# The opening of the first mixer: filter taps before the pool products, four small loads on ScalarE's queue, window sums by level, bias row added in the taps

## The reference, cut to what matters

```python
def pool_mixer(h, w, scale):                  # first mixer; h is the normed input
    for g, win in enumerate((2, 4, 8, 16)):   # 4 groups of 256 channels
        xg = hf[..., g * 256:(g + 1) * 256]
        cs = jnp.cumsum(xg, axis=1)
        lag = jnp.pad(cs[:, :-win], ((0, 0), (win, 0), (0, 0)))
        cnt = jnp.minimum(pos + 1, win)
        outs.append((cs - lag) / cnt - xg)
    pooled = jnp.stack(outs, axis=2)
    return jnp.einsum('blgc,gcd->blgd', pooled, w).reshape(B, L, 1024) * scale

def hyena_filters(L, w1, b1, w2, b2, freq, w3):   # depends on weights alone
    hid = jnp.sin(fr * (z @ w1 + b1))
    hid = jnp.sin(fr * (hid @ w2 + b2))
    h = (hid @ w3).reshape(L, 2, 2, 512)
    return h * decay[:, None, None, :]

def long_conv_bidir(u, h_fwd, h_bwd, bias):
    k2 = jnp.concatenate([h_fwd, zeros, h_bwd[:0:-1]], axis=0)
    K = jnp.fft.rfft(k2, n=2 * L, axis=0)         # the filter's spectrum
    ...
    return y + u * bias
```

## Time and profile before

| | us |
|---|---|
| median of 3 runs | 1048.89 (1047.71 to 1049.81) |
| the profiled execution | 1046.43 |
| its span, first to last instruction | 1044.7 |
| TensorE busy | 1004.6 (96%) |
| VectorE busy | 764.4 (73%) |
| ScalarE busy | 497.5 (48%) |
| GpSimd busy | 139.1 (13%) |
| mean granted clock | 0.985 |

### The profile page before, as it was taken

The page is one execution under the profiler, slowest core; times in us unless marked ns, Lnnn a source line. Parts: engine busy times, 40 slices in busy tenths (PEclk is TensorE's granted clock), DMA queues, the critical chain, the costliest instruction groups (busy, mean ns, idle before and its releaser), DMA issues.

```text
span 1044.7 us, 20358 instructions
## 1 busy us (share of the span) xinstructions
PE 1004.6 (96%) x7736; PEld 943.4 (90%) x7736; DVE 764.4 (73%) x1223; ACT 497.5 (48%) x728; POOL 139.1 (13%) x153
## 2 busy tenths in 40 slices
PE   5999999999999998999999999999999999999996
PEld 4379999999999988999999998987788999999996
DVE  6669888888866657998867765766455879866554
ACT  6355544444645534454444432564446555554441
POOL 4000000012000036300015400111110330000111
PEclk9699999999999998999999999999999999999998
DMA  7048777667733334566635632442233548644552
GB/s 250 1 161 290 264 271 259 204 240 246 251 123 122 122 104 159 201 240 238 229 127 192 228 127 86 164 145 91 100 123 122 185 176 296 249 163 173 167 178 84
DMA packets 38493, 186.80 MB, mean 179 GB/s; under 512 B 4936, under 2 KB 8809, under 8 KB 25578
## 3 DMA queue, kind: packets, MB, share of 16 engines
q1 hardware_dynamic: 38442, 186.09, 51.2%
HBM read 185.03 MB, written 1.05 MB: 178 GB/s over the span
## 4 chain that ended last, share of the span: by engine, by line
PE 87%; DVE 7%; ACT 2%; issue 2%; POOL 1%; DMA 0%; SPq 0%; DVEq 0%; ACTq 0%
PE ps L415 25%; PE ps L417 25%; PE ps L416 25%; DVE wl L356 2%; PE ps L1729 1%; PE ps L1997 1%; PE ps L1948 1%; PE ps L1738 1%; PE ps L1969 1%; PE ps L1957 1%; PE ps L1773 1%; PE ps L2022 1%; PE ps L2008 1%; DVE xl L1209 1%; ACT wh L350 1%
## 5 line engine op out<-in xcount | busy, mean ns | idle before, releaser
L415 PE MATMUL ps<-xh,wh 128*128 128x256 f32 (+3 forms) x1808 | 525.4, 291 | 11.3 <-DVE xl L1209 3.6
L417 PE MATMUL ps<-xl,wh 128*128 128x256 f32 (+3 forms) x1808 | 518.5, 287 | 0.0
L416 PE MATMUL ps<-xh,wl 128*128 128x256 f32 (+3 forms) x1808 | 517.7, 286 | 0.0
L356 DVE TENSOR_TENSOR wl<-stage,wh 128x1024 fp32r<-128x1024 f32 (+2 forms) x320 | 364.0, 1148 | 133.6 <-ACT wh L350 131.4
L350 ACT ACTIVATE wh<-stage 128x1024 fp32r<-128x1024 f32 (+2 forms) x320 | 306.6, 968 | 181.0 <-PE ps L417 148.3
L415 PEld LDWEIGHTS ps<-xh,wh 128*128 128x128 f32 x1808 | 342.9, 190 | 18.7 <-issue 6.4
L416 PEld LDWEIGHTS ps<-xh,wl 128*128 128x128 f32 x1808 | 342.9, 190 | 3.1 <-issue 1.4
L417 PEld LDWEIGHTS ps<-xl,wh 128*128 128x128 f32 x1808 | 341.4, 189 | 1.4
L415 PE MATMUL ps<-gh,wh 128*128 128x256 f32 (+1 forms) x528 | 150.1, 284 | 2.9 <-DVE wl L356 1.5
L416 PE MATMUL ps<-gh,wl 128*128 128x256 f32 (+1 forms) x528 | 149.4, 283 | 0.0
L417 PE MATMUL ps<-gl,wh 128*128 128x256 f32 (+1 forms) x528 | 148.9, 282 | 0.0
(11 more groups left out here) (247 smaller groups left out, 800.8 us busy)
## 6 DMA issues: line engine op xcount, KB each, us to landing
stage<-in_w_gu SPq DMA_DIRECT2D x66, 1024.0 KB, 4.8
stage<-in_w_dn SPq DMA_DIRECT2D x48, 704.0 KB, 4.1
adaw<-in_w_ada SPq DMA_DIRECT2D x48, 512.0 KB, 5.4
stage<-in_w_gates SPq DMA_DIRECT2D x8, 1024.0 KB, 5.0
stage<-in_w_hy SPq DMA_DIRECT2D x6, 1024.0 KB, 4.8
stage<-in_w_q SPq DMA_DIRECT2D x8, 512.0 KB, 4.8
stage<-in_w_k SPq DMA_DIRECT2D x8, 512.0 KB, 5.2
stage<-in_w_v SPq DMA_DIRECT2D x8, 512.0 KB, 5.2
```

Source lines behind the costliest of these rows:

```text
L356: nc.vector.tensor_tensor(wl[:, b, w], stage[:, b, w], wh[:, b, w].bitcast(fp32), ALU.subtract).then_inc(split_lo, 1)
L415: nc.tensor.matmul(psum, wh[:, b, w], xhi, start=first and n == 0, stop=False)
L416: nc.tensor.matmul(psum, wl[:, b, w], xhi, start=False, stop=False)
L417: last = nc.tensor.matmul(psum, wh[:, b, w], xlo, start=False, stop=close and n == len(blocks) - 1)
```

## The change

- The loads of zt, hw1, hpar and hw2 are issued by ACT at its start, in place of SP. On SP, par and hw3 move up ahead of the mixer's weights. The bias row and decay have a semaphore of their own.
- ACT loads the sine table first. The first sine stands between its two groups of four squares. The second sine stands before the last two weight splits of the mixer; the root follows it. Table loads in the opening go from 5 to 2.
- The second argument is made by DVE with the same 7 instructions as the first, after three of the eight xl instructions. ACT's scaling and POOL's ten instructions go; POOL has only wboth left, which now waits for hw3 alone.
- PE makes taps 0 to 3 before the mixer's tiles, which go to banks (m + 4) % 8; tiles 4 to 7 wait until DVE has read a tap's bank. Taps 4 to 7 follow, then the spectrum, of which parts 4 to 7 wait for all 8 taps to be read.
- The bias row is added where the taps of the second half of tokens are made (L1726, two matmuls in place of four), with an hzero that is zero but for its last column.
- DVE forms window sums for all groups that still need a level in one instruction: 8, 6, 4 and 2 tiles (window_sums), each followed by its group's pool_mixed. Taps 0 to 3 are read ahead of pool_scaled.
- gate_input and spectrum_stored alternate in another way on ACT; gate_input(6) and (7) stand behind spectrum_stored(7).

```diff
+            for dst, src in ((zt, "zt"), (hw1, "hw1"), (hpar, "hpar"), (hw2, "hw2")):
+                act.dma_start(dst[:, :], A[src]).then_inc(filter_in, 16)
+            act.preload_act_table(ACT.Sin)
+            for j in range(2):
+                act.wait_ge(h_in[j], 16)
+                for k in range(4 * j, 4 * j + 4):
+                    act.activation(squares0[:, k, :], h[:, k, :], ACT.Square).then_inc(sq0_ready, 1)
+                if j == 0:
+                    sine(0)
...
             for k in range(KD):
                 pool_input_hi(k)
...
+            for j in range(2):
+                hi_part("pool", 0, 0, j, first=True)
             sine(1)
             act.wait_ge(z_sin, 2)
-            act.activation(hzero[0:HD, :], hid[:, 1, TX - 1:TX].to_broadcast([HD, P]), ACT.Copy, scale=-1.0)\
-                .then_inc(hzero_hid, 1)
-            act.preload_act_table(ACT.Sqrt)
+            act.wait_ge(hzero_set, 2)
+            act.activation(hzero[0:HD, P - 1:P], hid[:, 1, TX - 1:TX], ACT.Copy, scale=-1.0).then_inc(hzero_hid, 1)
...
+            def window_sums(i):
+
+                k0, shift = 2 * i, 1 << i
+                width = TM + META - 2 * shift + 1
+                src, dst = (y0, sums_a, sums_b, sums_a)[i], (sums_a, sums_b, sums_a, sums_b)[i]
+                link(dve.tensor_tensor(dst[:, k0:KD, 0:width], src[:, k0:KD, 0:width],
+                                       src[:, k0:KD, shift:shift + width], ALU.add))
...
+            for k in range(3):
+                pool_input_lo(k)
+            sine_argument(1)
+            for k in range(3, KD):
                 pool_input_lo(k)
...
+            pe.wait_ge(wboth_set, 2)
+            pe.wait_ge(decay_in, 16 * 2)
+            pe.wait_ge(z_sin, 2)
+            pe.wait_ge(hzero_set, 2)
+            pe.wait_ge(hzero_hid, 1)
+            for i in range(4):
+                filter_taps(i)
...
-                last = products(ps[m][:, 0:TM], b, (2 * j, 2 * j + 1), wide(ALT, TM, 2 * g, 2 * g + 2))
+                if m >= 4:
+                    pe.wait_ge(f_read, m - 3)
+                last = products(ps[POOL_BANK(m)][:, 0:TM], b, (2 * j, 2 * j + 1), wide(ALT, TM, 2 * g, 2 * g + 2))
...
+            for i in range(4, 8):
+                pe.wait_ge(pool_read, i - 3)
+                filter_taps(i)
+            pe.wait_ge(const_in, 16 * 5)
+            pe.wait_ge(f_read, 4)
             for i in range(8):
+                if i < 4:
+                    pe.wait_ge(pool_read, i + 5)
+                else:
+                    pe.wait_ge(f_read, 8)
+                filter_spectrum(i)
```

More of the change, by code:

```diff
@@ L1223, in _ @@
                     lo_part("pool", 0, b, j)
-            inverse_root("pool", TM, 7)
+            dve.wait_ge(stats, STAT["pool"])
+            dve.tensor_scalar(stat[:, :], ps[7][:, 0:TM], 1.0 / D, EPS, ALU.mult, ALU.add).then_inc(mean_ready, 1)
+            dve.wait_ge(decay_in, 16 * 2)
+            taps(0)
+            dve.wait_ge(root_ready, ROOT["pool"])
+            link(dve.reciprocal(rstd[:, :], rstd[:, :]))
+            for i in range(1, 4):
+                taps(i)
             for m in range(KD):
@@ L1710, in _, with filter_taps @@
             ins.then_inc(stats, 1)
+            def filter_taps(i):
+                o, t, kind = i // 4, i // 2 % 2, i % 2
+                first = t == 1 and kind == 0
+                ins = pe.matmul(ps[i][:, :], hid[:, 1, t * P:(t + 1) * P], wboth[:, kind, o * HYW:(o + 1) * HYW],
+                                start=True, stop=not first)
+                if first:
+                    ins = pe.matmul(ps[i][:, :], hzero[:, :], hw3[:, (2 + o) * HYW:(3 + o) * HYW], start=False, stop=True)
+                ins.then_inc(f_out, 1)
@@ new lines, in filter_spectrum @@
+            def filter_spectrum(i):
+                o, part, f = i // 4, i // 2 % 2, i % 2
+                for t in range(2):
+                    ins = pe.matmul(ps[i][:, :], (cosf, sinf)[part][:, t, f * P:(f + 1) * P], gboth[:, o, part, t, :],
+                                    start=t == 0, stop=t == 1)
+                ins.then_inc(k_out, 1)
+            pe.wait_ge(wboth_set, 2)
+            pe.wait_ge(decay_in, 16 * 2)
+            pe.wait_ge(z_sin, 2)
+            pe.wait_ge(hzero_set, 2)
@@ L1733, in _ @@
-            pe.wait_ge(hzero_hid, 1)
-            for i in range(8):
-                o, part, f = i // 4, i // 2 % 2, i % 2
-                pe.wait_ge(f_read, 4 * o + 4)
-                for t in range(2):
-                    ins = pe.matmul(ps[i][:, :], (cosf, sinf)[part][:, t, f * P:(f + 1) * P], gboth[:, o, part, t, :],
-                                    start=t == 0, stop=part == 1 and t == 1)
-                if part == 0:
-                    ins = pe.matmul(ps[i][:, :], hzero[:, :], hw3[:, (2 + o) * HYW:(3 + o) * HYW], start=False, stop=True)
-                ins.then_inc(k_out, 1)
+            for i in range(4, 8):
+                pe.wait_ge(pool_read, i - 3)
+                filter_taps(i)
```

130 lines of the change are left out of this document (48 added, 82 removed).

## The result

| | before | after |
|---|---|---|
| median, us | 1047.68 (1045.86 to 1049.89, 12 runs) | 1051.03 (1049.40 to 1052.16, 12 runs) |
| the profiled execution | 1046.43 | 1050.16 |
| its span | 1044.7 | 1048.4 |
| PE's first matmul | 7.27 | 10.33 |
| first gu0 product | 64.83 | 69.86 |

The changed kernel is slower: the ratio of the times is 1.0030, with a 95% interval of 1.0021 to 1.0040. The forecast, 1045.9 with 1040.0 to 1049.8, has the wrong sign and doesn't hold the time. (The three runs of before that the prediction had were 1.2 above the median of twelve.)

The account below looks back on a forecast made before the run. PE, busy 96% of the span, was the bound, so the first gu0 product's start counts: 56.7 + 4.3 + 1.7 = 62.7, against an ordinary 65.7. Time: 1048.9 - 3.0 = 1045.9 us, range 1040 to 1049.8.

Parts of the forecast that it names:

- Small weights on ACT: Opening: with the four small loads issued by ACT, PE's first matmul comes at 5.5 instead of 7.27, at most 6.3.
- First argument, one clash of 2.4: PE's start to first sine: 1.24 plus 2.88, plus 2.4 of DVE waiting for one POOL wboth instruction.
- Up to the taps: First argument to first tap: second wboth blocks the first xl until 14.6; taps start at 19.5 instead of 28.0.
- The clock at taps and tiles: PE's clock falls to half 1 us into the taps and returns 2.4 into the tiles; DVE's scalings end 4.3 later.
- DVE's tail: DVE's window sums and tap reads after the scalings: 15.1 until tap 7 is read, at 46.1 with full clock.
- The wait that replaces the one removed: Middle of the spectrum: PE waits about 5 us for DVE's read of tap 7.
- From there: After tap 7's read: spectrum 4 to 7 takes 6.9, plus 1.7 for slow clock; sums 3.6.
- The sum: First gu0 product at 62.7 instead of an ordinary 65.7, so 3.0 us saved against the median.
- The slower one: Rival: small loads land at 7.3, hw3 still first, taps at 22 to 23 at half clock; gu0 68.5, 1051.7; chance 0.12.
- Gu0 as the measure: Start of the first gu0 product: each us by which it moves should move the kernel's end by one.

Follow-up runs that it names:

- filler: The changed kernel with five more 128-row matmuls, of no use to the result, in PE's idle time ahead of the taps; 1046.66 us, ratio to before 0.9994.
- taps_read_early: The changed kernel with DVE's reads of taps 4 to 7 moved right behind the mixer's first group; 1045.23 us, ratio to before 0.9976.
- small_first_on_sp: The changed kernel with the four small loads first on SP's queue, ahead of h; 1046.58 us, ratio to before 0.9994.
- small_back_on_sp: The changed kernel with the four small loads back on SP, behind h; 1051.02 us, ratio to before 1.0033.

## Why the prediction was wrong, point by point

- **Small weights on ACT: wrong, 4.8 us.** 5.5 was forecast, at most 6.3; measured 10.33. I took the time from issue to landing that the same loads had on SP, 4.17 from the last issue, as the upper bound; here it was 8.0 (2.34 to 10.33). No row before showed a load on a second queue beside a full one, and it should have been priced above SP's time too. The Trainium skill, "DMA: Bandwidth & Descriptors", section "Issuing engines are not separate DMA queues", has transfers of several engines interleave and only the time of issue saved. The trace agrees that they interleave, but not that this is all: with the same loads on SP the first matmul was 3.0 earlier (7.34), so moving them cost time.
- **First argument, one clash of 2.4: right.** From PE's start to the sine 16.81 - 10.33 = 6.5, and 1.24 + 2.88 + 2.4 = 6.5 was forecast. It was luck: hw3 landed at 10.2 rather than 8.8, and with PE at 7.34 two wboth stood in the way (4.1).
- **Up to the taps: the length right, one term not.** 7.5 from sine to taps forecast, 7.1 measured. Taps 23.95 instead of 19.5. I had the second wboth hold the first xl for 2.6. It had ended at 14.96, ahead of the sine; what held xl, for 2.26 until 19.04, was ACT's sine, squares and xh. That the two were nearly equal was luck.
- **The clock at taps and tiles: right in kind, 2.6 short.** It fell 0.3 us into the taps (1 forecast). But it came back only at 38.0, not 2.4 but 5.0 us into the tiles. First tap to last tile took 17.4; 14.8 was forecast (19.5 to 34.3), and 1.4 of the 2.6 are in the taps, 1.2 in the tiles. filler shows what the half clock costs there in all: 5.5 us at gu0, more than the 3.0 that I had forecast as the gain.
- **DVE's tail: right.** 15.1 from the first sum to the last tap read was forecast; 57.67 - 42.54 = 15.1. The sums took 2.55, 1.93, 1.32 and 0.72.
- **The wait that replaces the one removed: right.** About 5 forecast, 4.29 measured, ended by DVE's read of tap 7. taps_read_early prices it, with the slow rows behind it, at some 6.3.
- **From there: right.** 8.6 forecast for the rest of the spectrum, 8.67 measured; the sums 3.5.
- **The sum.** The step that failed is the first term, the landing of the small loads on ACT's queue: 10.33 in place of 5.5, of which 4.4 reached the taps. The second is the size of the clock's term. 62.7 + 4.4 (taps late) + 2.6 (clock) = 69.7, measured 69.86. The clock's terms alone would have eaten the gain (small_first_on_sp, with taps at 19.38: gu0 65.75, 1.8 more than forecast in taps and tiles and 1.35 more in the spectrum, no change in time); the landing made a loss of it.
- **The rivals.** The slower one has the mechanism, and small_back_on_sp is its case almost to the number: PE at 7.34 (7.3), gu0 68.61 (68.5), 1051.02 (1051.7). The changed kernel landed 3 us later still, and since that spared it one clash it lost only 1.3 more at gu0. I gave this rival 0.12, because I had bounded the landing from above by 6.3. With that bound gone it should have had far more.
- **Gu0 as the measure.** I let each us there move the end by one. Over the kernels here that holds to some 1.5 us.

## What to carry to other kernels

A few small loads that the first matmul waits for belong first on the queue that carries the bulk, not on a second queue beside it; the bulk then lands later, here by 2.2 us (ACT's squares at 6.83 instead of 4.67), which cost nothing here since the first sine could not have come before 8.3. Work moved into an engine's idle time gains little if the engine's clock falls there and the work is what another engine must read in between its own; the reads of a bank that a later matmul waits for should stand right where the bank is written. A helper on POOL that no longer waits for anything runs exactly when its data lands: ask which DVE instructions stand there.

## What the runs showed of the hardware

- Small transfers on ACT's queue were served late while SP's queue kept the 16 DMA engines full: the last of the four was issued at 2.34 and PE started at 10.33. With hw3 behind the mixer's weights instead of right behind h it was 8.13, with SP's queue left empty behind h and par 6.76; on SP's own queue behind h it was 7.34, and ahead of h 4.21.
- Beside POOL's 64x1024 addition of two SBUF operands, DVE's instructions on SBUF operands waited until POOL's instruction had ended, those with one input too (0.28 became 2.32). The one that read PSUM at 11.57 took 0.54 with wboth running since 10.27, the same 0.54 as without it at 8.58 in small_back_on_sp. The Trainium skill, "SBUF — State Buffer", section "Terms", calls the pair of ports that both engines share an exclusive lock which is held for the whole instruction; the rows agree.
- The 64-row taps ran at full clock (1.00, 2.4 GHz) throughout when PE was at full clock and busy up to them (filler: 2.84 for six records, two of which are a tap), and at 0.50 (1.2 GHz) for 14 us, without a return, where an idle stretch of 5.77 had stood ahead. A level that such work could not raise it could keep.
- The profile's granted clock can miss a stretch: in taps_read_early it reads 1.00 from 5 to 65 us, though six records of the taps took 5.46, as at 0.50 (5.45 in small_first_on_sp), and not 2.84.
